# DeltaNet stage of a two-layer hybrid backbone: doubling masks and beside-scaling issued on VectorE instead of GpSimd

## Chip, core and metric

One Trainium2 chip, one of its cores, one program of 38,510 profiled instructions. The metric is the device time of one execution in microseconds (us). Engines: TensorE (PE; its weight loads are PEld), VectorE (DVE), ScalarE (ACT), GpSimd (POOL), SyncE (SP).

## What is computed

The program is two layers of a mixed backbone over 256 latent tokens and 256 context tokens of width 1024: a half feed-forward, a token mixer, a second half feed-forward. The mixer adds three branches; the change is inside one of them, the bidirectional gated DeltaNet. All of its arithmetic is float32. The part that matters, cut from the reference:

```
m = jnp.where(strict, jnp.einsum('bhncd,bhnsd->bhncs', kb, k) * decay, 0.0)
eye = jnp.eye(DN_CHUNK, dtype=jnp.float32)
t_inv = lax.linalg.triangular_solve(eye + m, jnp.broadcast_to(eye, m.shape), left_side=True, lower=True)
u = jnp.einsum('bhncs,bhnse->bhnce', t_inv, v * beta[..., None])
w = jnp.einsum('bhncs,bhnsd->bhncd', t_inv, kb * jnp.exp(gam)[..., None])
...
v_new = u_c - jnp.einsum('bhcd,bhde->bhce', w_c, s)
```

There are 4 heads of dimension 128, two directions (`d` = 0 and 1), and per direction 4 tiles of 128 tokens. A tile holds two chunks of 64 tokens.

## The kernel before

The kernel is written engine by engine; every engine runs its own list in order, and semaphores (`wait_ge`, `then_inc`) tie the lists together. Nothing reorders them. In the DeltaNet stage nothing else of the network runs on TensorE: the stage is a loop over layer `l` (2) and tile step `j` (4), eight passes in all. I call each of the eight a pass; passes 1 to 4 are layer 0, passes 5 to 8 layer 1.

A pass inverts the unit-triangular matrix of a tile for 4 heads and both directions by doubling. `mt` is the masked product of keys with the decay, scaled by `beta`, in 64x64 blocks (128 partitions x 4 heads x 64 columns, so 256 elements in each partition). `X` is the inverse so far and `XT` its transpose. The constant `level` has 6 masks of 64 columns; mask 0 gives the first `X`, masks 1 to 5 pick out of `mt` what level `n` adds. For level `n` and direction `d`:

1. TensorE multiplies `level[d, n % 2]` (the masked `mt`, two buffers per direction) with `X` into PSUM (`TWO[d]`, called Y here; semaphore `y_made`), in `by_block`, 8 products of 64x64.
2. ScalarE copies Y to SBUF (L1075, `y_kept`).
3. TensorE multiplies `XT` with Y (`ONE[d]`, called XY here; `xy_made`).
4. VectorE subtracts XY from `X` (L2026, `x_ready`) and transposes `X` to `XT` (L2030, `xt_ready`).

TensorE's order in a level is Y of d=0, Y of d=1, XY of d=0, XY of d=1. After level 5 the block `beside` (the part of the tile's matrix between its two chunks, 64 partitions) joins the two 64-blocks, and the products with values and state follow.

VectorE begins a pass with, for each direction: L2007 twice and L2008 (products with the decay), L2010 (times `beta`, giving `mt`), L2012 (mask 0), L2015 (identity minus that), L2018 (transpose to `X`). Then come L2021 for both directions (`att`, which also frees the PSUM bank that XY of level 1 writes), then the levels. In levels 1 and 2 VectorE also does one L2042 each (`EG` times `qT`, 512 elements, both operands in SBUF).

GpSimd makes the five masked copies per direction (L772, 128x256, `level_ready`) and scales `beside` (L782, 64x256, twice, `beside_ready`). It starts when `mt_ready` comes and stays two levels ahead: the mask of level n goes into the buffer that Y of level n-2 has read. TensorE waits for both `level_ready` and `x_ready` in front of each Y.

All these tiles are views of one SBUF tensor, which the profile calls `work`; `cst` holds the constants and `small` holds `beta`. TensorE's stage instructions all have line L1538, the helper `mm`.

Of the kernel before, what the change touches and what calls it, by code (L numbers as in the profile page):

```python
# [31 lines left out]
P = 128  # L32
# [359 lines left out]
def backbone(nc, wts, par_d, cst_d, mod_d, x_d, c_d, out_d):  # L392
# [3 lines left out]
    with ExitStack() as ctx:  # L396
# [106 lines left out]
        def C(name, rows=slice(0, P)):  # L503
            at, n = CST[name]
            return cst[rows, at:at + n]
# [243 lines left out]
        @block.gpsimd  # L749
        def _(pool):  # L750
            pool.memset(eps, EPS).then_inc(eps_ready, 1)
            pool.memset(cond32[:, :, :], 0.0).then_inc(cond_zeroed, 1)
            pool.wait_ge(inputs_in, 16 * (DC + 2))
            for l in range(DEPTH):

                pool.wait_ge(att_kept, ATT[l] + width(l) // P * MH)
                for a in (0, 258):
                    last = pool.memset(convin[:, :, :, a:a + 2], 0.0)
                last.then_inc(borders_zeroed, 1)
                pool.memset(T_full[:, :, :], 0.0).then_inc(corners_zeroed, 1)  # L760
                for j in range(4):
                    it = l * 4 + j
                    for n in range(1, LEVELS):
                        for d in range(2):
                            if n == 1:
                                pool.wait_ge(mt_ready[d], it + 1)
                                for ready in beside_ready:
                                    pool.wait_ge(ready, it)
                            elif n > 2:
                                pool.wait_ge(y_made[d], it * LEVELS + n - 2)  # L770
                            mask = C("level")[:, n * BLOCK:(n + 1) * BLOCK].unsqueeze(1).to_broadcast([P, HEADS, BLOCK])
                            pool.tensor_tensor(level[:, d, n % 2, :, :], mt[:, d, :, :], mask,  # L772
                                               ALU.mult).then_inc(level_ready[d], 1)
                    for d in range(2):
                        rows = BEFORE[d]
                        factor = beta[rows, ORDER[d][j], 4 * d:4 * d + 4].unsqueeze(2).to_broadcast([BLOCK, HEADS, BLOCK])
                        pool.wait_ge(kk_read[d], it + 1)
                        for ready in level_ready:
                            pool.wait_ge(ready, (it + 1) * DEPTHS)
                        if d:  # L780
                            pool.wait_ge(beside_ready[0], it + 1)
                        pool.tensor_tensor(beside[rows, d, :, :], beside[rows, d, :, :], factor,  # L782
                                           ALU.mult).then_inc(beside_ready[d], 1)

        @block.scalar
        def _(act):
# [870 lines left out]
        def _(dve):  # L1657
# [156 lines left out]
            for l in range(DEPTH):  # L1814
# [175 lines left out]
                for j in range(4):  # L1990
                    it = l * 4 + j
                    tiles = [ORDER[d][j] for d in range(2)]
                    betas = [beta[:, tiles[d], 4 * d:4 * d + 4] for d in range(2)]
                    for d in range(2):
                        dve.wait_ge(decay_made[d], it + 1)
                        for hd in range(HEADS):
                            c = slice(hd * P, (hd + 1) * P)
                            last = stt(E[:, d, c], ONE[d][:, c], gam[:, d, tiles[d], hd:hd + 1],
                                       C("not_upto" if d == 0 else "not_from"), ALU.subtract, ALU.min)
                        last.then_inc(decay_masked[d], 1)  # L2000
                    for d in range(2):
# [14 lines left out]
                                XT[:, d, :, :], ALU.subtract))  # L2016
                        step.wait()
                        dve.transpose(X[:, d, :, :], XT[:, d, :, :]).then_inc(x_ready[d], 1)  # L2018
                    for d in range(2):
                        dve.wait_ge(kq_made[d], it + 1)  # L2020
                        tt(att[:, d, :], ONE[d][:, :], E[:, d, :], ALU.mult).then_inc(kq_read[d], 1)  # L2021
                    for n in range(1, LEVELS):
                        for d in range(2):
                            dve.wait_ge(xy_made[d], it * DEPTHS + n)
# [3 lines left out]
                            if n < LEVELS - 1:  # L2028
                                dve.wait_ge(x_ready[d], it * LEVELS + n + 1)
                                dve.transpose(XT[:, d, :, :], x).then_inc(xt_ready[d], 1)  # L2030
                            else:
                                if j == 0:
                                    dve.wait_ge(corners_zeroed, l + 1)
                                moved = ONE[d][:, HEADS * BLOCK:].rearrange("p (h c) -> p h c", h=HEADS)
                                for rows in (LOW, HIGH):
                                    last = tt(heads(T_full[rows, d, :])[:, :, rows], XT[rows, d, :, :], moved[rows, :, :],
                                              ALU.subtract)
                                last.then_inc(xt_ready[d], 1)
                        if n < 3:
                            d = n - 1  # L2040
                            dve.wait_ge(gain_exp[d], it + 1)
# [113 lines left out]
```

## Time and profile before

| | |
|---|---|
| median of 3 runs | 2859.64 us (2858.6 to 2860.43) |
| the profiled execution | 2859.57 us |
| its span, first to last instruction | 2857.8 us (1.8 us lie around it) |
| busy: PE, PEld | 2644.8 us (93%), 2095.4 us (73%) |
| busy: DVE, ACT, POOL | 1388.5 us (49%), 994.3 us (35%), 80.3 us (3%) |
| mean granted TensorE clock | 0.952 of full |

"Busy" is time in which an instruction was running on the engine, over its span. A row of the time line reads: start, duration, engine, line, operation, output and inputs, shape, count of merged instructions, and in brackets how long the engine idled before it and who released it. An instruction with no bracket followed its forerunner with no idle time that the profile counts.

### The profile page before, as it was taken

How to read it: one execution, taken by the hardware profiler on the slowest of the kernel's cores; microseconds unless marked ns; L12 is line 12 of the kernel's file. 1: busy time of each engine (PE TensorE's matmuls, PEld its weight loads, DVE VectorE, ACT ScalarE, POOL GpSimd, SP SyncE). 2: the span in 40 equal slices, each digit the busy share in tenths (PEclk: the TensorE clock that was granted, in tenths of full speed). 3: DMA queues.
4: the chain of work that ended last, by engine and by line, in shares of the span. 5: the costliest groups of instructions: out<-in, count | busy, mean ns of one | idle time of the engine just before them, and what ended most of it. 6: DMA issues, size and time to landing. Idle time of an engine off the chain costs nothing.

```text
span 2857.8 us, 38510 instructions
## 1 busy us (share of the span) xinstructions
PE 2644.8 (93%) x16344; PEld 2095.4 (73%) x16344; DVE 1388.5 (49%) x2092; ACT 994.3 (35%) x1541; POOL 80.3 (3%) x108
## 2 busy tenths in 40 slices
PE   4999998989978899989999989999898977889999
PEld 2777777634758877767777768888663767889899
DVE  4333344336776663363332353333435677656654
ACT  2322223323563332223222132222241564344443
POOL 0000000000002200000000000000000002200000
PEclk6999999988988999999999999999997988999999
DMA  5444442100210023424444432222220120024454
GB/s 228 177 177 171 158 157 103 60 30 1 89 59 2 2 90 132 147 74 165 168 169 161 161 126 89 103 96 98 87 89 30 60 74 16 2 101 167 169 185 163
DMA packets 44665, 309.79 MB, mean 108 GB/s; under 512 B 5072, under 2 KB 6224, under 8 KB 7632
## 3 DMA queue, kind: packets, MB, share of 16 engines
q1 hardware_dynamic: 44208, 306.20, 29.2%
q8 instruction: 131, 2.15, 0.3%
q10 hardware_dynamic: 288, 1.14, 0.1%
q14 instruction: 38, 0.31, 0.0%
HBM read 306.27 MB, written 1.05 MB: 108 GB/s over the span
## 4 chain that ended last, share of the span: by engine, by line
PE 84%; DVE 10%; ACT 3%; issue 2%; DMA 1%; SPq 0%; DVEq 0%; ACTq 0%
PE bank L1235 65%; PE bank L1538 7%; PE bank L1251 2%; PE bank L1228 2%; DVE rt L1677 2%; PE bank L1462 2%; PE bank L1484 1%; PE bank L1286 1%; DVE w_lo L1666 1%; DMA ring<-in_wts 1%; PE bank L1264 1%; ACT L816 1%; PE bank L1421 1%; PE bank L1471 1%; DVE u_lo L1706 1%
## 5 line engine op out<-in xcount | busy, mean ns | idle before, releaser
L1666 DVE TENSOR_TENSOR w_lo<-ring,w_hi 128x1024 fp32r<-128x1024 f32 x420 | 511.1, 1225 | 1034.5 <-ACT w_hi L798 1031.3
L1235 PE MATMUL bank<-u_hi,w_hi 128*128 128x512 f32 (+1 forms) x2208 | 818.2, 371 | 83.9 <-DVE w_lo L1666 46.7
L1235 PE MATMUL bank<-u_hi,w_lo 128*128 128x512 f32 (+1 forms) x2208 | 801.8, 363 | 0.0
L1235 PE MATMUL bank<-u_lo,w_hi 128*128 128x512 f32 (+1 forms) x2208 | 799.6, 362 | 0.0
L798 ACT ACTIVATE w_hi<-ring 128x1024 fp32r<-128x1024 f32 x420 | 441.4, 1058 | 956.6 <-PE bank L1235 656.2
L1235 PEld LDWEIGHTS bank<-u_hi,w_hi 128*128 128x128 f32 x2208 | 423.1, 192 | 182.0 <-issue 85.4
L1235 PEld LDWEIGHTS bank<-u_hi,w_lo 128*128 128x128 f32 x2208 | 423.4, 192 | 64.0 <-issue 3.9
L1235 PEld LDWEIGHTS bank<-u_lo,w_hi 128*128 128x128 f32 x2208 | 422.8, 191 | 64.1
L1538 PE MATMUL bank<-work 64*64 64x64 f32 (+1 forms) x3952 | 234.6, 248 | 37.7 <-DVE work L2018 21.4
L1235 PE MATMUL bank<-hidden_hi,w_hi 128*128 128x512 f32 (+1 forms) x704 | 259.3, 368 | 0.0
L1538 PEld LDWEIGHTS bank<-work 64*64 64x64 f32 (+1 forms) x3952 | 222.0, 161 | 49.8 <-POOL work L772 31.7
L1235 PE MATMUL bank<-hidden_lo,w_hi 128*128 128x512 f32 (+1 forms) x704 | 258.2, 367 | 0.0
L1235 PE MATMUL bank<-hidden_hi,w_lo 128*128 128x512 f32 (+1 forms) x704 | 257.7, 366 | 0.0
L1235 PEld LDWEIGHTS bank<-hidden_hi,w_hi 128*128 128x128 f32 x704 | 132.2, 188 | 28.6 <-issue 4.9
L1235 PEld LDWEIGHTS bank<-hidden_lo,w_hi 128*128 128x128 f32 x704 | 132.1, 188 | 24.0
L1235 PEld LDWEIGHTS bank<-hidden_hi,w_lo 128*128 128x128 f32 x704 | 132.3, 188 | 23.6
L1677 DVE RECIPROCAL rt<-rt 128x512 f32<-128x512 f32 (+1 forms) x34 | 104.3, 3067 | 55.3 <-ACT rt L816 55.3
L1251 PE MATMUL bank<-ring,cond 128*32 128x256 f32 x1152 | 83.6, 411 | 21.1 <-DMA ring<-in_wts 21.1
L850 ACT ACTIVATE hidden_hi<-sg 128x512 fp32r<-128x512 f32 (+1 forms) x88 | 50.7, 578 | 132.8 <-DVE sg L1772 132.7
L857 ACT ACTIVATE sg<-bank 128x512 f32<-128x512 f32 (+1 forms) x88 | 46.7, 535 | 116.4 <-PE bank L1235 116.3
L772 POOL TENSOR_TENSOR work<-work,cst 128x256 f32<-128x256 f32 x80 | 68.0, 867 | 417.9 <-DVE work L2010 398.0
L1251 PEld LDWEIGHTS bank<-ring,cond 128*32 128x32 f32 x1152 | 31.6, 114 | 64.1 <-issue 32.4
(190 smaller groups left out, 2523.3 us busy)
## 6 DMA issues: line engine op xcount, KB each, us to landing
ring<-in_wts SPq DMA_DIRECT2D x288, 1024.0 KB, 4.8
h<-in_x SPq DMA_DIRECT2D x8, 256.0 KB, 11.1
par<-in_par ACTq DMA_DIRECT2D x2, 556.0 KB, 5.7
out<-h SPq DMA_DIRECT2D x8, 128.0 KB, 4.0
cst<-in_cst SPq DMA_DIRECT2D x1, 911.5 KB, 10.7
mod_par<-in_mod SPq DMA_DIRECT2D x1, 96.0 KB, 10.0
cond<-in_c SPq DMA_DIRECT2D x1, 8.0 KB, 1.7
```

The costliest lines, as they stand in the source:

```text
L772: pool.tensor_tensor(level[:, d, n % 2, :, :], mt[:, d, :, :], mask, ALU.mult).then_inc(level_ready[d], 1)
L798: act.activation(w_hi[:, b % HALVES, :], half_source(n % RING, part), ACT.Copy).then_inc(weights_rounded, 1)
L816: act.activation(rt[rows, n % 2, 0:w], bank[4 + n % 2][rows, 0:w], ACT.Sqrt, bias=eps[rows, :], scale=1.0 / size).then_inc(roots, 1)
L850: act.activation(h_hi[:, 2 * i + c, 0:w], sg[:, c, 0:w], ACT.Copy).then_inc(hidden_rounded, 1)
L857: act.activation(sg[:, c, 0:w], bank[(q0 + c) % 4][:, 0:w], ACT.Silu).then_inc(drained["a"], 1)
L1228: last = weights.used(pe.matmul(out, lhsT, rhs, start=n == 0, stop=n == len(parts) - 1))
L1235: last = weights.used(pe.matmul(out, lhs[a], rhs[b], start=start and n == 0, stop=stop and n == 2))
L1251: last = pe.matmul(bank[7 - unit % 2][32 * j:32 * j + 32, 0:256], cond32[:, k, :], panel[:, kk, j, :], start=k == 0, stop=k == DC - 1)
L1462: pe.matmul(bank[S_BANKS[a % 4]][:, 0:keys.stop - keys.start], qq[0:QK, hd, t * P:(t + 1) * P], kk[0:QK, hd, keys], start=True, stop=True) ...
L1538: return pe.matmul(out, lhsT, rhs, start=start, stop=stop)
L1666: tt(w_lo[:, b % HALVES, :], half_source(n % RING, part), w_hi[:, b % HALVES, :].bitcast(F32), ALU.subtract).then_inc(panel_left[n % RING] ...
L1677: step(dve.reciprocal(r, r))
```

## The change

GpSimd's whole loop over the passes is taken out. VectorE gets a helper `mask_level(d, n)` that makes the same masked copy, and calls it ten times a pass: masks 1 and 2 before level 1, mask n+2 after VectorE's work of level n (n = 1, 2, 3). The two scalings of `beside` come after VectorE's work of level 4. No other engine's list changes. The rest of the numbers, buffers and semaphores is as before. Line numbers behind the cut are lower in the changed kernel, so L2012, L2015, L2018, L2021, L2026, L2030 and L2042 of before are L1997, L2000, L2003, L2007, L2013, L2017 and L2037 there, and the masks are L1975.

```
@@ gpsimd, in the loop over l
-                for j in range(4):
-                    it = l * 4 + j
-                    for n in range(1, LEVELS):
-                        for d in range(2):
-                            if n == 1:
-                                pool.wait_ge(mt_ready[d], it + 1)
-                                for ready in beside_ready:
-                                    pool.wait_ge(ready, it)
-                            elif n > 2:
-                                pool.wait_ge(y_made[d], it * LEVELS + n - 2)
-                            mask = C("level")[:, n * BLOCK:(n + 1) * BLOCK].unsqueeze(1).to_broadcast([P, HEADS, BLOCK])
-                            pool.tensor_tensor(level[:, d, n % 2, :, :], mt[:, d, :, :], mask,
-                                               ALU.mult).then_inc(level_ready[d], 1)
-                    for d in range(2):
-                        rows = BEFORE[d]
-                        factor = beta[rows, ORDER[d][j], 4 * d:4 * d + 4].unsqueeze(2).to_broadcast([BLOCK, HEADS, BLOCK])
...
-                        pool.tensor_tensor(beside[rows, d, :, :], beside[rows, d, :, :], factor,
-                                           ALU.mult).then_inc(beside_ready[d], 1)
@@ vector, in the loop over j
+                    def mask_level(d, n):
+                        if n > 2:
+                            dve.wait_ge(y_made[d], it * LEVELS + n - 2)
+                        tt(level[:, d, n % 2, :, :], mt[:, d, :, :],
+                           C("level")[:, n * BLOCK:(n + 1) * BLOCK].unsqueeze(1).to_broadcast([P, HEADS, BLOCK]),
+                           ALU.mult).then_inc(level_ready[d], 1)
@@
                         dve.transpose(X[:, d, :, :], XT[:, d, :, :]).then_inc(x_ready[d], 1)
+                        mask_level(d, 1)
                     for d in range(2):
                         dve.wait_ge(kq_made[d], it + 1)
                         tt(att[:, d, :], ONE[d][:, :], E[:, d, :], ALU.mult).then_inc(kq_read[d], 1)
+                        mask_level(d, 2)
                     for n in range(1, LEVELS):
@@ after both directions of level n
+                        for d in range(2):
+                            if n + 2 < LEVELS:
+                                mask_level(d, n + 2)
+                            elif n == 4:
+                                rows = BEFORE[d]
+                                tt(beside[rows, d, :, :], beside[rows, d, :, :],
+                                   betas[d][rows, :].unsqueeze(2).to_broadcast([BLOCK, HEADS, BLOCK]),
+                                   ALU.mult).then_inc(beside_ready[d], 1)
```

The first place is VectorE's list in pass 1 for direction 1, up to the first subtraction of level 1. Before:

```order
L2007 TENSOR_TENSOR work<-bank,work 64x256 [waits decay_exp1,kk_made1]
L2007 TENSOR_TENSOR work<-bank,work 64x256
L2008 TENSOR_TENSOR work<-bank,work 64x256
L2010 TENSOR_TENSOR work<-work,small 128x256 [waits dve_step]
L2012 TENSOR_TENSOR work<-work,cst 128x256 [waits mt_ready1]
L2015 TENSOR_TENSOR work<-cst,work 128x256 [waits dve_step]
L2018 STREAM_TRANSPOSE work<-work 128x256 [waits dve_step]
L2021 TENSOR_TENSOR work<-bank,work 128x512 [waits kq_made0]
L2021 TENSOR_TENSOR work<-bank,work 128x512 [waits kq_made1]
L2026 TENSOR_TENSOR work<-work,bank 128x256 [waits xy_made0]
```

The same place in VectorE's list of the changed kernel (the first row is direction 0's mask 1):

```order
L1975 TENSOR_TENSOR work<-work,cst 128x256
L1992 TENSOR_TENSOR work<-bank,work 64x256 [waits decay_exp1,kk_made1]
...
L2003 STREAM_TRANSPOSE work<-work 128x256 [waits dve_step]
L1975 TENSOR_TENSOR work<-work,cst 128x256
L2007 TENSOR_TENSOR work<-bank,work 128x512 [waits kq_made0]
L1975 TENSOR_TENSOR work<-work,cst 128x256
L2007 TENSOR_TENSOR work<-bank,work 128x512 [waits kq_made1]
L1975 TENSOR_TENSOR work<-work,cst 128x256
L2013 TENSOR_TENSOR work<-work,bank 128x256 [waits xy_made0]
```

A mask now stands ahead of direction 1's first product, one behind its transpose, and one behind each of the two `att` products.

The second place is VectorE's list from level 1's second transpose to level 2's last operation. Before:

```order
L2030 STREAM_TRANSPOSE work<-work 128x256 [waits x_ready1]
L2042 TENSOR_TENSOR work<-work 128x512 [waits gain_exp0]
L2026 TENSOR_TENSOR work<-work,bank 128x256 [waits xy_made0]
L2030 STREAM_TRANSPOSE work<-work 128x256 [waits x_ready0]
L2026 TENSOR_TENSOR work<-work,bank 128x256 [waits xy_made1]
L2030 STREAM_TRANSPOSE work<-work 128x256 [waits x_ready1]
L2042 TENSOR_TENSOR work<-work 128x512 [waits gain_exp1]
```

The same place in the changed kernel:

```order
L2017 STREAM_TRANSPOSE work<-work 128x256 [waits x_ready1]
L1975 TENSOR_TENSOR work<-work,cst 128x256 [waits y_made0]
L1975 TENSOR_TENSOR work<-work,cst 128x256 [waits y_made1]
L2037 TENSOR_TENSOR work<-work 128x512 [waits gain_exp0]
L2013 TENSOR_TENSOR work<-work,bank 128x256 [waits xy_made0]
L2017 STREAM_TRANSPOSE work<-work 128x256 [waits x_ready0]
L2013 TENSOR_TENSOR work<-work,bank 128x256 [waits xy_made1]
L2017 STREAM_TRANSPOSE work<-work 128x256 [waits x_ready1]
L1975 TENSOR_TENSOR work<-work,cst 128x256 [waits y_made0]
L1975 TENSOR_TENSOR work<-work,cst 128x256 [waits y_made1]
L2037 TENSOR_TENSOR work<-work 128x512 [waits gain_exp1]
```

Two masks stand between the second transpose and the next level's first subtraction, and in levels 1 and 2 the 512-element product stands there as well.

## Rows read from the trace of the kernel before

**Rows 1.** The page: busy time by engine, and the chain that ended last.

```profile
PE 2644.8 (93%) x16344; PEld 2095.4 (73%) x16344; DVE 1388.5 (49%) x2092; ACT 994.3 (35%) x1541; POOL 80.3 (3%) x108
...
PE 84%; DVE 10%; ACT 3%; issue 2%; DMA 1%; SPq 0%; DVEq 0%; ACTq 0%
```

**Rows 2.** Busy time by stretch: the DeltaNet stages of layers 0 and 1.

```profile
855.00:1006.00 151.00, 129.80 (x2065) 122.86 (x2065) 94.78 (x222) 56.08 (x148) 38.82 (x48) 0.92 0.01 2
2370.00:2520.00 150.00, 127.88 (x2041) 120.10 (x2042) 94.47 (x220) 58.41 (x151) 38.88 (x48) 0.92 0.03 9
```

**Rows 3.** Time line of pass 3, from the first mask to level 1.

```profile
934.75 0.42 DVE L2012 TENSOR_TENSOR work<-work,cst 128x256 f32<-128x256 f32 x1
934.79 0.96 POOL L772 TENSOR_TENSOR work<-work,cst 128x256 f32<-128x256 f32 x1 [23.93 <-DVE work L2010]
935.21 0.83 DVE L2015 TENSOR_TENSOR work<-cst,work 128x256 f32<-128x256 f32 x1
...
936.59 0.57 PEld L1538 LDWEIGHTS bank<-work 64*64 64x64 f32 x16 [1.21 <-POOL work L772]
...
939.43 0.45 DVE L2018 STREAM_TRANSPOSE work<-work 128x256 f32<-128x256 f32 x1
939.91 1.29 DVE L2021 TENSOR_TENSOR work<-bank,work 128x512 f32<-128x512 f32 x2
939.95 0.61 PEld L1538 LDWEIGHTS bank<-work 64*64 64x64 f32 x16 [2.79 <-POOL work L772]
```

**Rows 4.** VectorE's time line of pass 3: ends of levels 1 to 4.

```profile
943.58 0.65 DVE L2042 TENSOR_TENSOR work<-work 128x512 f32<-128x512 f32 x1
944.79 0.42 DVE L2026 TENSOR_TENSOR work<-work,bank 128x256 f32<-128x256 f32 x1 [0.56 <-PE bank L1538]
...
946.40 1.00 DVE L2042 TENSOR_TENSOR work<-work 128x512 f32<-128x512 f32 x1
947.33 0.42 DVE L2026 TENSOR_TENSOR work<-work,bank 128x256 f32<-128x256 f32 x1
...
949.87 0.42 DVE L2026 TENSOR_TENSOR work<-work,bank 128x256 f32<-128x256 f32 x1 [0.85 <-PE bank L1538]
...
952.88 0.42 DVE L2026 TENSOR_TENSOR work<-work,bank 128x256 f32<-128x256 f32 x1 [1.32 <-PE bank L1538]
```

**Rows 5.** Single lines over all eight passes: duration ns, min/median/max.

```profile
L2015 DVE TENSOR_TENSOR work<-cst,work x16: 826/831/836, 861.3 to 2489.3; 128x256 f32<-128x256 f32 x16
...
L2042 DVE TENSOR_TENSOR work<-work x16: 650/995/1171, 869.8 to 2496.9; 128x512 f32<-128x512 f32 x16
...
L772 POOL TENSOR_TENSOR work<-work,cst x80: 719/814/1176, 860.9 to 2497.4; 128x256 f32<-128x256 f32 x80
```

**Rows 6.** VectorE's time line, end of level 1 in passes 1, 6, 7 and 8.

```profile
871.54 0.42 DVE L2026 TENSOR_TENSOR work<-work,bank 128x256 f32<-128x256 f32 x1 [1.11 <-PE bank L1538]
...
2422.35 1.17 DVE L2042 TENSOR_TENSOR work<-work 128x512 f32<-128x512 f32 x1
...
2456.69 1.08 DVE L2042 TENSOR_TENSOR work<-work 128x512 f32<-128x512 f32 x1
...
2494.37 1.03 DVE L2042 TENSOR_TENSOR work<-work 128x512 f32<-128x512 f32 x1
2495.32 0.41 DVE L2026 TENSOR_TENSOR work<-work,bank 128x256 f32<-128x256 f32 x1
```

**Rows 7.** TensorE's line L1538: until whom its engine sat idle (us, times).

```profile
  POOL work L772: 39.9, 24
  DVE work L2018: 21.4, 8
```

**Rows 8.** Stretches of level 1 in pass 1 and level 2 in pass 3; the clock is the third from the end.

```profile
866.10:869.00 2.90, 2.90 (x54) 2.90 (x56) 2.07 (x5) 0.38 (x1) 2.06 (x3) 0.50 0.00 0
...
944.00:946.50 2.50, 2.40 (x68) 2.11 (x66) 1.87 (x6) 0.78 (x3) 1.88 (x3) 1.00 0.00 0
```

More of the change, by code:

```diff
@@ L760, in _ @@
                 pool.memset(T_full[:, :, :], 0.0).then_inc(corners_zeroed, 1)
-                for j in range(4):
-                    it = l * 4 + j
-                    for n in range(1, LEVELS):
-                        for d in range(2):
-                            if n == 1:
-                                pool.wait_ge(mt_ready[d], it + 1)
-                                for ready in beside_ready:
-                                    pool.wait_ge(ready, it)
-                            elif n > 2:
-                                pool.wait_ge(y_made[d], it * LEVELS + n - 2)
-                            mask = C("level")[:, n * BLOCK:(n + 1) * BLOCK].unsqueeze(1).to_broadcast([P, HEADS, BLOCK])
-                            pool.tensor_tensor(level[:, d, n % 2, :, :], mt[:, d, :, :], mask,
-                                               ALU.mult).then_inc(level_ready[d], 1)
-                    for d in range(2):
-                        rows = BEFORE[d]
-                        factor = beta[rows, ORDER[d][j], 4 * d:4 * d + 4].unsqueeze(2).to_broadcast([BLOCK, HEADS, BLOCK])
[L777 to L781, printed above, removed]
-                        pool.tensor_tensor(beside[rows, d, :, :], beside[rows, d, :, :], factor,
-                                           ALU.mult).then_inc(beside_ready[d], 1)
         @block.scalar
```

## Prediction

> **What bounds the kernel now.** I read the page first, for the bound: TensorE is busy 93% of the span and carries 84% of the chain that ended last; GpSimd is busy 80 us, 3% [rows 1]. So the DeltaNet stage matters only through what TensorE waits for. The view by stretches gives its size: some 150 us in each layer, TensorE busy 130 and 128 of them, VectorE 95 and 94, ScalarE 56 and 58, GpSimd 39 in each, at almost no DMA [rows 2]. Nothing from outside runs beside it, so whatever a pass gains or loses goes straight into the time.
>
> Then the time line of one pass, for what a pass waits for. In its first part TensorE has nothing to do but to wait for VectorE: it starts Y of direction 1 at 939.95, when the transpose L2018 has ended at 939.88 [rows 3]. In the levels the loop is a chain through three engines: subtraction L2026, Y, ScalarE's copy, XY, next L2026. At full clock one turn takes 947.33 - 944.79 = 2.54 us and again 949.87 - 947.33 = 2.54 us [rows 4]. VectorE's own work in a turn (two subtractions, two transposes) leaves it 0.85 us idle ahead of the next L2026, and 1.32 us ahead of level 5's [rows 4]. This idle time is the cover of what the change adds. In levels 1 and 2 the 512-element product L2042 sits in it already: at level 2 nothing is left (L2026 at 947.33 has no idle time before it), at level 1 0.56 us [rows 4].
>
> **The chip's behaviour that the price rests on.** L2012 and L2015 have the same size, 128x256 with both inputs in SBUF. L2012 takes 0.42 us, L2015 0.83 us in all 16 cases (826 to 836 ns) [rows 3, 5]. L2012 starts 0.04 us ahead of GpSimd's mask, L2015 in the middle of it. The mask then takes 0.96 us, where its shortest is 0.719 [rows 3, 5]. The picture: one of the two waits for the other. L2042 fits: 0.65 us where it starts 0.09 us ahead of GpSimd's next pair, up to 1.17 us elsewhere [rows 4, 5, 6]. So I take it that without GpSimd L2015 costs 0.42 and L2042 0.65.
>
> The Trainium skill says the same in "SBUF — State Buffer", section "Who interferes with whom": a VectorE instruction with two SBUF inputs takes its second one through a read interface that it shares with GpSimd, and whoever issues first keeps it. The trace agrees: 0.42 against 0.83.
>
> A mask on VectorE has L2012's form exactly, hence 0.42 us. Where neither needs the other's result, an operation starts about 0.08 us before its forerunner ends: two L2021 take 1.29 us together, and L2026 starts at 947.33 while L2042 ends at 947.40 [rows 3, 4]. No mask is needed by its neighbour, so each takes 0.345 us of VectorE's time, a pair 0.69.
>
> **The change, part by part** (per pass; eight passes).
>
> *GpSimd's list removed.* It frees nothing that is waited for. The trace names L772 as the releaser of TensorE's 24 waits of 39.9 us [rows 7], but the masks were out earlier: direction 1's at about 939.12 (0.96 behind 938.16), TensorE went on at 939.95, just behind L2018; direction 0's mask ended at 935.75, TensorE started at 936.59 [rows 3]. What is gained is the contention: 0.41 us for each L2015 and up to 0.52 for L2042.
>
> *First part.* Direction 0's work loses 0.41 (L2015) and gains a mask of 0.345: direction 1 starts 0.06 us earlier. Again 0.41 against 0.345 for direction 1, so Y of direction 1 comes some 0.13 us earlier. But mask 2 of direction 0 stands ahead of direction 1's `att` product, which frees the bank of direction 1's XY: this ends 0.2 us later than now, and TensorE, which works in order, gives part of the 0.13 back. I book half of 8 x 0.12 us: **-0.5 us**.
>
> *Level 1 to 2.* Two masks are put between the second transpose and the next L2026. In passes 1, 2 and 5 TensorE runs at half clock there (0.50, that is 1.2 GHz [rows 8]) and VectorE idles 1.11 us [rows 6], more than 0.69: nothing. In passes 3 and 4 0.56 us are idle [rows 4]; 0.69 less 0.56 and less the overlap of 0.08 is 0.05 each. In passes 6 to 8 no idle time is left, but L2042 falls from 1.17, 1.08 and 1.03 to 0.65 [rows 6]: 0.69 x 3 - (0.52 + 0.43 + 0.38) = 0.74. Together **+0.8 us**.
>
> *Level 2 to 3.* No idle time in any pass. Masks +0.69, L2042 from 1.00 to 0.65 [rows 4]: +0.34 each, **+2.7 us**. Late by it are L2026 and all that follows in the pass.
>
> *Levels 3 to 4 and 4 to 5.* 0.69 us of masks under 0.85 idle. The two scalings of `beside` have 64 partitions and 256 elements; no VectorE row of this form is shown, the nearest is a mask, 0.42 us, and even with no overlap 0.9 us lie under 1.32 [rows 4]. TensorE needs `beside` only after level 5. Nothing. If the cover were gone they would cost 0.69 and 0.9 a pass.
>
> *Waits.* The new wait on `y_made` is for a Y whose copy is long made when VectorE reaches the mask (its XY has already been subtracted), so nothing queues behind it. No DMA moves.
>
> Sum: -0.5 + 0.8 + 2.7 = +3.0 us. Against the profiled execution's own 2859.57 us (span 2857.8 and 1.8 around it), which lies 0.07 under the median, this gives **2862.6 us**, +0.1%. A measurement of this kernel can tell about 0.2%, 5.7 us, from no change.
>
> The bounds of the unknown terms: first part -1.0 (Y's lead kept) to 0; a mask 0.345 to 0.45 of VectorE's time; L2015 and L2042 between their two observed durations. That is what the rivals price.
>
> **Rivals.**
>
> *A. No overlap: each mask costs 0.45 us* (0.42 and a gap of 0.03 as from 935.17 to 935.21 [rows 3]). For it: every operation that waits for its forerunner has this gap. Against: masks don't. First part 8 x 2 x (0.45 - 0.41) = 0.6; level 1 to 2: 2 x (0.90 - 0.56) + 3 x 0.90 - 1.33 = 2.1; level 2 to 3: 8 x (0.90 - 0.35) = 4.4; level 3 to 4: 8 x 0.05 = 0.4. Sum +7.5: 2867.1 us, slower. It decides from about 0.42 us per mask on.
>
> The Trainium skill has a rule for it: "VectorE: DVE Perf Modes", section "The DRAIN you can't avoid", says that the next operation doesn't start until the pipe is empty, though the section on two instructions with no wait between them lets some start earlier. The trace speaks for the second: 1.29 us for two operations of 0.69.
>
> *B. The long L2015 and L2042 are not GpSimd's doing.* For it: 831 ns is strikingly constant. Against: GpSimd's mask stands at the same place each time, and L2042 varies between 650 and 1171 ns. Then nothing pays for the masks: first part 8 x 0.69, level 2 to 3 8 x 0.69, level 1 to 2 2 x 0.13 + 3 x 0.69 = 13.4 us: 2873.0 us, slower.
>
> *C. TensorE did wait for GpSimd's masks*, as the profile names it [rows 7]. Then its 16 waits of level 1 shrink by 0.96 - 0.42 = 0.54 us each, -8.6 us: 2851.0 us, faster. Against it are the end times worked out above.
>
> *D. The clock moves.* The half clock of level 1 costs pass 1 about 0.65 - 0.08 + 1.11 = 1.68 us of VectorE's slack instead of 0.85, so 0.83 us; the same in passes 2 and 5, and 0.56 + 0.57 - 0.85 = 0.28 in passes 3 and 4. When the passes shift, these low stretches may fall elsewhere: if all went away -3.1 us, while the masks of level 1 would then show in passes 1 to 5 too (5 x 0.34 less the 0.1 booked): 2859.57 + 3.0 - 3.1 + 1.6 = 2861.1 us, or 2859.6 if they don't. The opposite, all eight as low as pass 1, costs 5 x 0.83 - 2 x 0.28 = 3.6 and hides the 0.8 of level 1: 2865.4 us.
>
> **How the numbers follow.** My forecast 0.66 (its own range 2860.5 to 2865), D 0.12, A 0.10, B 0.07, C 0.05. The range goes from 2857.8 to 2868.0: it holds the forecast, nearly all of D and most of A, and leaves out B, C and the edges, 0.2. Faster by over 0.2% is C, 0.05, and some 0.01 of D; slower by over 0.2% is A and B, 0.17; within 0.2% 0.77.
>
> **What the profile after would show.** L2000 (was L2015) at about 0.42 us: right on contention; at 0.83: B. L2037 (was L2042) at 0.65. Masks at 0.38 to 0.42 us, their starts 0.35 apart; 0.45 apart: A. From level 2's first subtraction to level 3's 2.88 us instead of 2.54, then 2.54 again. TensorE's Y of direction 1 about 5.1 us behind L1997's start of direction 0, now 5.20; at 4.6 or less C is right. I would be wrong if VectorE's queue were late in levels 3 or 4 as well, or if the granted clock of the stages left 0.92 by more than 0.02.

## The result and the profile after

The changed kernel takes 2863.9 us (median of 20 runs) against 2859.09 us; the ratio is 1.0016, 95% interval 1.0009 to 1.0023, so 4.6 us slower, between 2.6 and 6.6. One run of each kernel took far longer (3365.81 and 6534.54 us); the ratio leaves them out. The forecast was +3.0 us, with 2857.8 to 2868.0 as its range. The traced execution took 2865.29 us at the same mean clock as before, 0.952.

The page's rows on the engines and on the chain, which answer to [rows 1]:

```profile
PE 2647.8 (92%) x16344; PEld 2095.5 (73%) x16344; DVE 1409.6 (49%) x2188; ACT 994.6 (35%) x1541; POOL 2.6 (0%) x12
...
PE 82%; DVE 11%; ACT 3%; issue 2%; DMA 1%; SPq 0%; DVEq 0%; ACTq 0%
```

VectorE has 21 us more work, GpSimd 78 us less. TensorE's share of the chain fell by two points, VectorE's rose by one. The two stages by stretches, as [rows 2]:

```profile
855.00:1006.00 151.00, 128.67 (x2066) 120.70 (x2066) 105.84 (x270) 56.20 (x147) 0.00 (x0) 0.94 0.01 2
2370.00:2520.00 150.00, 127.40 (x2020) 118.93 (x2021) 106.10 (x270) 56.65 (x146) 0.00 (x0) 0.89 0.03 9
```

The clock is third from the end: 0.94 in layer 0's stretch and 0.89 in layer 1's, both 0.92 before. This is the first sign that the clock has a part in it. But the program comes to layer 1's stage 3.7 us later now, so the same stretch holds more of the half-clock time that lies ahead of it. From the first mask of pass 5 to the last level of pass 8 the two kernels differ by 0.01 only, before first:

```profile
2380.18:2503.40 123.22, 104.55 (x1841) 98.09 (x1842) 85.62 (x199) 47.56 (x128) 38.88 (x48) 0.93 0.01 2
```

```profile
2383.87:2508.80 124.93, 105.97 (x1842) 99.29 (x1842) 95.86 (x247) 47.58 (x128) 0.00 (x0) 0.92 0.01 2
```

The single lines over all passes (ns, min/median/max), as [rows 5]. L2000 is the identity minus mask 0 (L2015 before), L2037 the 512-element product (L2042 before), L1975 the masks:

```profile
L2000 DVE TENSOR_TENSOR work<-cst,work x16: 424/424/427, 861.8 to 2493.6; 128x256 f32<-128x256 f32 x16
...
L2037 DVE TENSOR_TENSOR work<-work x16: 681/685/686, 870.7 to 2502.6; 128x512 f32<-128x512 f32 x16
...
L1975 DVE TENSOR_TENSOR work<-work,cst x80: 381/398/417, 862.6 to 2505.1; 128x256 f32<-128x256 f32 x80
```

With GpSimd gone the strange 831 ns are 424, in all 16 cases, and the product no longer varies between 650 and 1171. That speaks for the two engines having been in each other's way; the experiments below test it.

VectorE's time line of pass 3, first part, as [rows 3]:

```profile
934.35 0.42 DVE L1997 TENSOR_TENSOR work<-work,cst 128x256 f32<-128x256 f32 x1
934.80 0.42 DVE L2000 TENSOR_TENSOR work<-cst,work 128x256 f32<-128x256 f32 x1
935.26 0.45 DVE L2003 STREAM_TRANSPOSE work<-work 128x256 f32<-128x256 f32 x1
935.63 0.38 DVE L1975 TENSOR_TENSOR work<-work,cst 128x256 f32<-128x256 f32 x1
935.94 0.86 DVE L1992 TENSOR_TENSOR work<-bank,work 64x256 f32<-64x256 f32 x2
...
939.33 0.69 DVE L2007 TENSOR_TENSOR work<-bank,work 128x512 f32<-128x512 f32 x1
```

A mask takes 0.31 us of VectorE's time (935.63 to 935.94), not 0.345. The first `att` product starts 4.98 us behind mask 0, before it was 5.16. And the levels of the same pass, as [rows 4]:

```profile
943.09 0.72 DVE L1975 TENSOR_TENSOR work<-work,cst 128x256 f32<-128x256 f32 x2
943.72 0.68 DVE L2037 TENSOR_TENSOR work<-work 128x512 f32<-128x512 f32 x1
944.67 0.42 DVE L2013 TENSOR_TENSOR work<-work,bank 128x256 f32<-128x256 f32 x1 [0.27 <-PE bank L1515]
...
946.28 0.71 DVE L1975 TENSOR_TENSOR work<-work,cst 128x256 f32<-128x256 f32 x2
946.92 0.68 DVE L2037 TENSOR_TENSOR work<-work 128x512 f32<-128x512 f32 x1
947.52 0.41 DVE L2013 TENSOR_TENSOR work<-work,bank 128x256 f32<-128x256 f32 x1
...
950.05 0.42 DVE L2013 TENSOR_TENSOR work<-work,bank 128x256 f32<-128x256 f32 x1 [0.21 <-PE bank L1515]
```

Level 2 to 3 takes 947.52 - 944.67 = 2.85 us instead of 2.54, with no idle time ahead of the subtraction: VectorE is the bound there. Level 3 to 4 is at 2.53 again and has 0.21 us left of the 0.85.

The rest can be counted by starts on VectorE's time line. From the start of mask 0 (direction 0) to the first subtraction of level 5, summed over the eight passes, I get (us):

| | before | after |
|---|---|---|
| mask 0 to level 1 | 57.8 | 56.0 |
| level 1 to 2 | 24.2 | 25.2 |
| level 2 to 3 | 20.3 | 22.8 |
| level 3 to 5 | 44.4 | 44.3 |
| sum | 146.6 | 148.2 |

The passes explain +1.6 us. The spans differ by 5.7. Of this 0.45 us lie ahead of the first mask (which starts at 860.86 us before and 861.31 after), where the two programs are the same; traces of kernels that are the same up to there put it anywhere from 858.75 to 861.61 us, so this is scatter. From the first mask to the end it is 2002.2 us against 1996.9, so +5.3. The rest lies outside of the passes, and most of it in one place: from the first mask of pass 4 to that of pass 5, through the end of layer 0 and the first part of layer 1, where the two kernels do the same work in the same order, it takes 2383.87 - 972.72 = 1411.15 us, and before 2380.18 - 972.55 = 1407.63. The rows of these four starts, the kernel before first:

```profile
972.55 0.42 DVE L2012 TENSOR_TENSOR work<-work,cst 128x256 f32<-128x256 f32 x1
...
2380.18 0.43 DVE L2012 TENSOR_TENSOR work<-work,cst 128x256 f32<-128x256 f32 x1
```

After:

```profile
972.72 0.42 DVE L1997 TENSOR_TENSOR work<-work,cst 128x256 f32<-128x256 f32 x1
...
2383.87 0.42 DVE L1997 TENSOR_TENSOR work<-work,cst 128x256 f32<-128x256 f32 x1
```

Going through this stretch instruction by instruction (ScalarE's records stand in the same order in both), the distance between the traces is constant to 0.1 us (leaving out the copies of weights, which run ahead and swing) but for these places: near 2073 us the changed kernel gains 0.26, near 2217 to 2220 it loses 1.2, near 2328 to 2345 it loses 1.7, and near 2367 another 0.5. At the first of the losses, TensorE's time line of the kernel before:

```profile
2217.05 0.66 PE L1471 MATMUL bank<-cst,work 128*128 128x128 f32 x4
2217.54 1.02 PE L1462 MATMUL bank<-work 96*128 96x512 f32 x2
2218.74 0.66 PE L1471 MATMUL bank<-cst,work 128*128 128x128 f32 x4 [0.17 <-DVE work L1925]
```

And of the kernel after:

```profile
2217.33 1.12 PE L1448 MATMUL bank<-cst,work 128*128 128x128 f32 x4
2218.24 1.91 PE L1439 MATMUL bank<-work 96*128 96x512 f32 x2
2219.94 1.06 PE L1448 MATMUL bank<-cst,work 128*128 128x128 f32 x4
```

The same four products (the first row) take 1.12 us instead of 0.66. The stretches tell why, before first, then after (span, TensorE's busy time, clock, DMA):

```profile
2205.00:2217.00 12.00, 8.03 (x12) 0.50 0.01 1
2217.60:2220.40 2.80, 2.58 (x15) 1.00 0.01 3
```

```profile
2205.00:2217.00 12.00, 8.02 (x12) 0.50 0.00 0
2217.60:2220.40 2.80, 2.80 (x9) 0.50 0.00 0
2222.00:2232.00 10.00, 10.00 (x57) 1.00 0.00 0
```

Both come out of a thin stretch at half clock (0.50, 1.2 GHz: small products between VectorE's roots and rotations) into the attention. Before, the clock is back at full (2.4 GHz) by 2217.6 us, as the attention's first heads run; after, it is still at half to 2220.4 and full only in the next stretch shown. In the traces' clock records this half clock begins at 2176.07 us before and 2176.52 after, and it ends at 2217.03 and 2220.89.

### The profile page after: what moved, and what is told of

The parts are those of the page before. It is cut to its first block, busy times and chain, and to the rows that moved or that the text cites. A ratio compares the mean times of both kernels' runs of the same rounds, so it can differ in the third digit from the quotient of the medians.

```text
span 2863.5 us, 38468 instructions
## 1 busy us (share of the span) xinstructions
PE 2647.8 (92%) x16344; PEld 2095.5 (73%) x16344; DVE 1409.6 (49%) x2188; ACT 994.6 (35%) x1541; POOL 2.6 (0%) x12
## 4 chain that ended last, share of the span: by engine, by line
PE 82%; DVE 11%; ACT 3%; issue 2%; DMA 1%; SPq 0%; DVEq 0%; ACTq 0%
PE bank L1212 65%; PE bank L1515 6%; PE bank L1228 2%; PE bank L1205 2%; DVE rt L1654 2%; PE bank L1439 2%; PE bank L1461 1%; PE bank L1263 1%; DVE w_lo L1643 1%; DMA ring<-in_wts 1%; PE bank L1241 1%; DVE work L2013 1%; PE bank L1448 1%; ACT L793 1%; PE bank L1398 1%
## 5 line engine op out<-in xcount | busy, mean ns | idle before, releaser
L1749 DVE TENSOR_TENSOR sg<-sg,bank 128x512 f32<-128x512 f32 (+1 forms) x88 | 54.0, 617 | 49.4 <-PE bank L1212 49.4
```

Source lines behind the costliest of these rows:

```text
L1749: tt(sg[:, c, 0:w], sg[:, c, 0:w], bank[(q0 + 2 + c) % 4][:, 0:w], ALU.mult).then_inc(drained["v"], 1)
```

## The experiments

The theories. **Q**: the passes decide, VectorE's queue in levels 1 and 2 costs and the end of the contention gains. **S**, later sharper as **L**: the larger part of the loss is the granted clock outside the stage, decided by some tenths of a microsecond in when the program comes to a place. **A**, the rival of L, says that times just add: a delay costs what it lasts. Every run is compared with runs of the kernel before on the same chip.

**The changed kernel again, unchanged.**

> The changed kernel once more, unchanged, to have it beside the others on one chip and to see in a second trace what the eight passes add and what lies outside of them. Theory Q (VectorE's queue in levels 1 and 2 is the cost, contention the gain): the eight passes, from the first mask to level 5's first subtraction, sum to 148 us again (before: 146.6), and level 2 to 3 takes 2.84 us in each. Theory S (the time is lost outside the stage, where stretches of low clock fall otherwise): the part outside of the passes differs from the first trace's by 2 us or more either way. Time: 1.0010 to 1.0023 of before.

1.0018 of before (1.0010 to 1.0027). The passes sum to 148.3 us, level 2 to 3 takes 2.84 to 2.88 in each. And the part outside repeats as well: pass 4 to pass 5 takes 1411.13 us. The two traces' spans differ by 1.55 us, all of it ahead of the first mask; from there to the end both take 2002.2 us. So the loss is no accident of one execution, as theory S had it, but belongs to the program.

**The 512-element products behind level 5**, in the changed kernel:

```
-                        if n < 3:
-                            d = n - 1
-                            dve.wait_ge(gain_exp[d], it + 1)
...
+                    for d in range(2):
+                        dve.wait_ge(gain_exp[d], it + 1)
+                        tt(heads(EG[:, d, :]), ..., ALU.mult).then_inc(gain_ready[d], 1)
                     for d in range(2):
                         dve.wait_ge(fresh_made[d], it + 1)
```

> The changed kernel, with VectorE's two 512-element products (EG times qT) moved from levels 1 and 2 to behind level 5, where VectorE idles 5 us. Theory Q: level 2 to 3 falls from 2.84 to 2.54 us in all eight passes and level 1 to 2 from 2.94 to about 2.6 where the clock is full; 8 x 0.3 + 5 x 0.3 = -4 us against the changed kernel, so about 1.0000 to 1.0005 of before. Theory S: the turns shorten in the same way, but the time stays within 1.5 us of the changed kernel.

1.0011 (1.0002 to 1.0020). Its time line of pass 3:

```profile
942.79 0.42 DVE L2013 TENSOR_TENSOR work<-work,bank 128x256 f32<-128x256 f32 x1 [1.03 <-PE bank L1515]
...
944.40 0.72 DVE L1975 TENSOR_TENSOR work<-work,cst 128x256 f32<-128x256 f32 x2
945.33 0.42 DVE L2013 TENSOR_TENSOR work<-work,bank 128x256 f32<-128x256 f32 x1 [0.21 <-PE bank L1515]
```

Level 2 to 3 is 2.54 us again (2.58 in pass 5), and the passes sum to 145.4 us, 1.2 less than before: inside the stage this kernel beats the old one, as Q says. The step was smaller than Q had it, 2.8 us and not 4, since level 1 to 2 gave 0.6 and not 1.5. Its time is still 0.11% above it, and pass 4 to pass 5 takes 2382.77 - 970.56 = 1412.21 us. Of its two expectations on the time the one of theory S came nearer: the medians are 1.2 us apart (2862.23 and 2863.45). From the first mask to the end the traces differ by 2.0.

**The same move in the kernel before**, with GpSimd still making the masks (the same edit, on the old kernel).

> The kernel before, GpSimd still makes the masks, with the same two products moved behind level 5. It tells whether they alone cost anything. Theory Q: level 2 to 3 was at 2.54 us with them and stays there; level 1 to 2 loses the 0.1 to 0.2 us that three passes lay above it; first part unchanged, L2015 still 0.83 us: -0.5 us, 0.9998 of before. A rival of it (the products cost in the kernel before as well): -2 us or more.

0.9999 (0.9990 to 1.0008), passes 146.5 us (0.1 less, where 0.5 was expected), pass 4 to 5 1407.66. The products were covered as long as the masks were elsewhere; at level 2 to 3 only both together cost.

**Mask 1 on VectorE, the others on GpSimd, products late.**

```
-                    for n in range(1, LEVELS):
+                    for n in range(2, LEVELS):
                         for d in range(2):
-                            if n == 1:
-                                pool.wait_ge(mt_ready[d], it + 1)
+                            if n == 2:
+                                pool.wait_ge(level_ready[d], it * DEPTHS + 1)
...
                         dve.transpose(X[:, d, :, :], XT[:, d, :, :]).then_inc(x_ready[d], 1)
+                        tt(level[:, d, 1, :, :], mt[:, d, :, :],
+                           C("level")[:, BLOCK:2 * BLOCK].unsqueeze(1).to_broadcast([P, HEADS, BLOCK]),
+                           ALU.mult).then_inc(level_ready[d], 1)
```

> VectorE makes only mask 1 (behind its transpose to X), GpSimd masks 2 to 5 and the scaling of beside, starting mask 2 when mask 1 is out; the 512-element products behind level 5. So no operation of VectorE with two SBUF inputs should meet GpSimd in the first part. Theory Q: the first operation after mask 0 falls from 0.83 to 0.42 us, first part 7.15 to 7.24 before, now 7.0; levels 2.54 us at full clock. Sum over eight passes about -1.5 to -2.5 us, 0.9992 to 0.9996 of before. If the 0.83 us were not contention it stays and the first part grows by 0.7 us.

1.0014 (1.0005 to 1.0023), where a gain was expected: a miss on the time. In the stage the contention went as written, and the first part takes 7.0 us:

```profile
932.85 0.42 DVE L2012 TENSOR_TENSOR work<-work,cst 128x256 f32<-128x256 f32 x1
933.31 0.42 DVE L2015 TENSOR_TENSOR work<-cst,work 128x256 f32<-128x256 f32 x1
...
934.60 0.72 POOL L772 TENSOR_TENSOR work<-work,cst 128x256 f32<-128x256 f32 x1 [25.99 <-DVE work L2019]
```

L2015 is at 0.42 us though GpSimd still makes masks, since it no longer makes one at that moment, and GpSimd's mask is at 0.72 instead of 0.96. The passes sum to 145.3 us, 1.3 less than before, a little short of the 1.5 expected at least. But pass 4 to 5 takes 2383.30 - 971.08 = 1412.22. Three kernels with 1411 to 1412, two with 1407.6: time for theory L.

**0.4 us of delay added to the changed kernel**, once, in layer 1:

```
                     dve.wait_ge(roots, n + 1)
+                    if l and kind == "q":
+                        for _ in range(2):
+                            step(dve.tensor_copy(small[:, 206:207], eps))
+                            step.wait()
```

> The changed kernel with 0.3 to 0.4 us of idle work added once: two copies of one column to an unused place, one after the other, on VectorE in layer 1 ahead of the reciprocal of the query roots (about 2174.8 us), where TensorE waits for VectorE. Theory L (the place of the program against the chip's changes of TensorE's clock decides over some 3 us: the traces of all kernels with masks on VectorE come to this point 0.25 to 0.4 us earlier against the clock's edges than before, and lose 1.1 us each at about 2220, 2330 and 2367): the three steps go, the time FALLS by about 2.8 us, to 1.0007 of before. Theory A (times just add): it grows by 0.4 us.

1.0009 (1.0000 to 1.0018), from 1.0018: with work added it came down, and pass 4 to 5 takes 2378.35 - 971.30 = 1407.05 us, 4.1 less than without the copies. Not all of this is gain: the passes sum to 149.4 us, 1.1 more, with more turns at half clock. From the first mask to the end it is 3.3 less. TensorE's row at the attention's start has the short form again:

```profile
2216.93 0.66 PE L1448 MATMUL bank<-cst,work 128*128 128x128 f32 x4
```

**The same delay in the kernel with the late products.**

> The kernel with the 512-element products behind level 5, with the same two copies. Theory L: 3.1 us less than without them, about the time of before (0.9998 to 1.0003). Theory A: 0.4 us more, 1.0012 of before.

0.9998 (0.9989 to 1.0007), from 1.0011; pass 4 to 5 1409.03 us, 3.2 less (3.3 from the first mask to the end).

**0.3 us of work left out of the kernel before**, at the same place (it leaves 48 of the 256 query roots of layer 1 uninverted):

```
-                    dve.reciprocal(r, r).then_inc(head_roots_inverted, 1)
+                    cut = r[:, 0:208] if l and kind == "q" else r
+                    dve.reciprocal(cut, cut).then_inc(head_roots_inverted, 1)
```

> The kernel before, with 0.3 us of work left out at the same place: VectorE's reciprocal of the query roots in layer 1 takes 208 of the 256 columns (the last 48 tokens' roots stay uninverted). Theory L: coming 0.3 us earlier to the clock's edge costs the three steps, the time GROWS by about 2.9 us to 1.0010 of before, with less work. Theory A: 0.3 us less.

1.0011 (1.0002 to 1.0020), with less work and untouched passes (146.7 us). Pass 4 to 5 takes 2381.75 - 970.99 = 1410.76 us, 3.1 more than before (3.3 from the first mask to the end). The attention's second group of four products, in TensorE's time line, has the long form (1.06 us, before 0.66 at 2218.74):

```profile
2217.84 1.06 PE L1471 MATMUL bank<-cst,work 128*128 128x128 f32 x4
```

**The delay in the kernel with mask 1 on VectorE.**

> The kernel with mask 1 on VectorE, masks 2 to 5 on GpSimd and the late products, with the same two copies. Theory L: 2.8 to 3.1 us less than without them, 0.9998 to 1.0003 of before. Theory A: 0.4 us more.

1.0001 (0.9992 to 1.0010), from 1.0014; pass 4 to 5 1407.99 us, 4.2 less (3.5 from the first mask to the end).

**The delay in the kernel before**, as a control.

> The kernel before with the two small copies alone (ahead of the reciprocal of the query roots in layer 1). A control for the runs with them: here the three steps at 2220, 2330 and 2367 us aren't there to begin with. Theory L (place against the clock's edges): nothing to win, 0.3 to 0.4 us more, 1.0001 of before. If the copies themselves did something good, it would fall here too, by 2 us or more.

1.0002 (0.9994 to 1.0011), pass 4 to 5 1408.68, passes 145.8 us; from the first mask to the end 0.1 more than before. The copies do nothing good by themselves.

The traces of all runs can be sorted by one number: how long behind the fall of the clock near 2176 us the attention's first four products start. In six traces it is 40.95 to 41.26 us (the kernel before, as it is, with the late products and with the delay, and the three other kernels with the delay), and there the half clock lasts 40.96 us. In seven it is 40.60 to 40.83 us (the changed kernel twice, its late products, mask 1 on VectorE, the shorter reciprocal, `beside` alone and the contention put back, both told below), and there the half clock lasts 44.37 us. None of the thirteen is out of line. The doubled masks, the last run below, stand apart: the fall itself comes at another place of the program there (39.85 us, and the half clock lasts 40.96).

**Only the scaling of `beside` on VectorE.** GpSimd keeps all its masks; its last loop goes and VectorE gets the two products behind level 4, as in the change.

> One part alone: only the two scalings of beside are made by VectorE (behind level 4), GpSimd still makes all masks. Theory Q: nothing in the passes, level 4 to 5 stays at 3.01 us, first part 7.15 to 7.24. Whether layer 1's mixer comes earlier against the clock's edges I can't say beforehand: if any longer list of VectorE does that, the time is 1.0010 of before, if only the shorter passes do, it is 1.0000.

1.0010 (1.0001 to 1.0020). The passes are those of before (146.8 us). Pass 4 to 5 takes 2382.68 - 971.84 = 1410.84 us. Eight instructions in each layer, all hidden, moved from GpSimd's list to VectorE's, cost most of what the whole change costs (the medians are 3.8 us apart, 5.1 with the whole change). It begins 145 us ahead of the attention, at the last rows of the norm that feeds layer 1's mixer. VectorE's time line of the kernel before:

```profile
2071.19 0.88 DVE L1706 SCALAR_TENSOR_TENSOR u_lo<-sq,mods,u_hi 128x256 fp32r<-128x256 f32 x2
2072.67 0.88 DVE L1706 SCALAR_TENSOR_TENSOR u_lo<-sq,mods,u_hi 128x256 fp32r<-128x256 f32 x2 [0.60 <-ACT u_hi L836]
2073.47 1.22 DVE L1666 TENSOR_TENSOR w_lo<-ring,w_hi 128x1024 fp32r<-128x1024 f32 x1
```

And of the kernel with `beside` alone, where the idle time is 0.25 instead of 0.60:

```profile
2070.46 0.88 DVE L1694 SCALAR_TENSOR_TENSOR u_lo<-sq,mods,u_hi 128x256 fp32r<-128x256 f32 x2
2071.59 0.88 DVE L1694 SCALAR_TENSOR_TENSOR u_lo<-sq,mods,u_hi 128x256 fp32r<-128x256 f32 x2 [0.25 <-ACT u_hi L824]
```

The kernel before, and the three with VectorE's list unchanged in length up to here (late products, shorter reciprocal, delay alone), all show 0.60 or 0.61. All ten traces of kernels with more instructions on VectorE ahead of this place show 0.25 or 0.26. It is a wait of 0.35 us that they don't have, at an instruction that has nothing to do with the change. The same ten also have fewer instructions on GpSimd, and no run separates the two.

The DMA records give a lead. In the four traces with the wait, the instruction behind it is the 1600th of VectorE's records, and a transfer of instructions (8 KB, queue 14) starts 0.67 to 0.70 us behind its start. In all 14 traces such a transfer comes when VectorE has started 1597 to 1601 of them, so with 8 instructions more it lies 2.1 us ahead of this place, with 48 or more 47 us and farther. The rows of the transfer, first of the kernel before (window 2073.3 to 2073.5 us), then of `beside` alone (2069.4 to 2069.6):

```profile
q14 instruction: 1, 0.01, 17.8%
```

```profile
q14 instruction: 1, 0.01, 12.5%
```

So the wait stands where VectorE's own list comes to a block of instructions, and the length of that list moves it away. That a fetch costs the 0.35 us is inferred from the place; no run with instructions added on VectorE alone tests it.

**Contention put back into the changed kernel**:

```
+                for j in range(4):
+                    for d in range(2):
+                        if l + j + d:
+                            pool.wait_ge(unused_made, 8 * l + 2 * j + d)
+                        pool.wait_ge(mt_ready[d], 4 * l + j + 1)
+                        pool.tensor_tensor(unused[:, :], C("level")[:, 0:256], C("level")[:, 64:320],
+                                           ALU.mult).then_inc(unused_made, 1)
```

> The changed kernel, with GpSimd given one useless product of 128x256 constants (both inputs in SBUF, into an unused place) for each direction, started by mt_ready as its first mask was before. It takes no data from the stage and nobody waits for it. Theory Q: VectorE's operation after mask 0 is back from 0.42 to 0.83 us, and the first part of a pass from 7.03 to about 7.8 us; 8 x 0.8 = +6.4 us less what the clock hides, against the changed kernel. Rival B of the prediction (the long time is not GpSimd's doing): 0.42 and 7.03 stay.

1.0042 (1.0029 to 1.0054), an estimated 7 us above the changed kernel's 1.0018, where 6.4 were expected. The first part takes 7.81 to 7.87 us, the passes 156.0 in sum, 7.7 more than the changed kernel's:

```profile
934.44 0.42 DVE L2006 TENSOR_TENSOR work<-work,cst 128x256 f32<-128x256 f32 x1
934.55 0.92 POOL L768 TENSOR_TENSOR unused<-cst 128x256 f32<-128x256 f32 x1 [35.14 <-DVE work L2004]
934.90 0.85 DVE L2009 TENSOR_TENSOR work<-cst,work 128x256 f32<-128x256 f32 x1
```

GpSimd's product shares no data and no semaphore that VectorE waits for with L2009, and L2009 is back at 0.85 us. The Trainium skill has the rule in "SBUF — State Buffer", section "Who interferes with whom": a VectorE instruction with two inputs in SBUF takes the second one through a read interface that it shares with GpSimd, and the order of issue decides who waits. The trace agrees: L2006, which started first, keeps its 0.42.

**Masks behind level 3 made twice**, in the changed kernel (two more products of the same kind ahead of them).

> The changed kernel with both masks behind level 3 made twice. There 0.85 us were idle before, and two masks take 0.69 of them. Theory Q with 0.345 us per mask: four masks take 1.38 us, less the overlap of 0.08 that is 1.30, so level 3 to 4 goes from 2.53 to 2.99 us. With 0.45 us per mask (rival A): 3.4 us.

One run, 2866.98 us. Level 3 to 4 takes 2.91 us in all passes:

```profile
950.09 0.72 DVE L2028 TENSOR_TENSOR work<-work,cst 128x256 f32<-128x256 f32 x2
950.72 0.75 DVE L1975 TENSOR_TENSOR work<-work,cst 128x256 f32<-128x256 f32 x2
951.39 0.42 DVE L2013 TENSOR_TENSOR work<-work,bank 128x256 f32<-128x256 f32 x1
```

Four masks take 951.39 - 950.09 = 1.30 us, 0.325 each. The turn was expected at 2.99 us by this price and at 3.4 by rival A's 0.45, which is out.

## Why the prediction came out right, point by point

The sum was right in its sign and near in size, but partly for another reason than the one it gave. Measured, by its own terms:

*First part*, booked at -0.5 us: -1.8. L2015 fell by 0.41 as written, but a mask behind a transpose takes 0.31 us of VectorE's time and not 0.345, and TensorE gave nothing of the lead back: the first `att` product comes 0.18 us earlier, the first subtraction 0.22. The term was mis-sized: half of the gain was taken off without a row that showed it, and the mask's price was too high. The mechanism holds.

*Level 1 to 2*, booked at +0.8: +1.0. The split by passes was not as written, since the half clock moved to other passes (3, 5 and 8 instead of 1, 2 and 5).

*Level 2 to 3*, booked at +2.7: +2.5, 2.84 us against the 2.88 foreseen. The move of the products to behind level 5 takes this term away entirely, which shows that it is the queue of masks and product together. The product went to 0.685 us, not to 0.65.

*Levels 3 to 5*, booked at nothing: -0.1. The cover of 0.85 held, with 0.21 to spare, and the doubled masks show that it is a cover: some 0.6 us more of work cost 0.38.

*GpSimd's list is waited for by nobody* (against rival C): right. TensorE starts Y of direction 1 at 939.36, 5.01 us behind the first mask; 5.20 before, 5.1 foreseen, 4.6 or less by rival C.

So the passes gave +1.6 us where I had +3.0, and the whole came to +4.6: that the sum lies near the measured time is in part luck, two errors of opposite sign. The step that failed is this one: "Nothing from outside runs beside it, so whatever a pass gains or loses goes straight into the time." It doesn't. Between the starts of pass 4 and pass 5 the changed kernel loses 3.5 us, only 0.2 of it in pass 4 and the rest on unchanged work, the same in a second trace, by the clock. I had the clock as rival D, with a chance of 0.12, for the passes alone. It acted mostly outside the stage, and there it repeats. The runs with 0.4 us of delay show it: three kernels became faster with it (by 0.0009, 0.0013 and 0.0013 of the time), one kernel became slower by 0.0011 with 0.3 us of work less, and the control stayed. In the three pairs with the delay the intervals of the times overlap; the traces settle it, with 3.3, 3.3 and 3.5 us less from the first mask to the end, 3.3 more with the shorter reciprocal and 0.1 more in the control. The prediction's own warning, a stage whose clock leaves 0.92 by more than 0.02, came up in the fixed stretch of layer 1 (0.89), but mostly because the stretch held other work; counted from the first mask it is 0.92 against 0.93.

The chain is then: another split of the instructions over VectorE and GpSimd, a wait of 0.35 us gone at 2072 us, the mixer of layer 1 0.26 us earlier, the clock back at full 3.4 us later in the program at the attention's start, 3.4 us lost there and in the two places after it. The links behind the second are shown by the delays and the shorter reciprocal; the first is shown only as a pattern over the kernels, with the transfer of instructions at VectorE's 1600th as the likely reason of the wait. Outside of this stretch and the passes +0.35 us are left behind level 5 of pass 8, not explained. Nor are the passes' +1.6 all queue: layer 0's came out at -0.1 and layer 1's at +1.7 with the same work. Layer 0 has two turns of level 1 at half clock before and one after, layer 1 one before and two after (3.43 and 3.46 us each, against 2.6 to 3.0 at full clock). At 0.5 to 0.7 us for each such turn, an estimate from these rows, about 0.9 us of the 1.8 between the layers are the clock's; no run separates the rest.

Rival B is refuted by 424 ns in all 16 cases and by the contention put back, rival A by the doubled masks, rival C by the 5.01 us. One slip of the prediction's sums: rival D's second case is 2859.57 + 3.0 - 3.1 = 2859.5, not 2859.6.

None of the versions beats the kernel before beyond what the measurement can tell: the best are 0.9998 and 1.0001, the one with late products and the one with mask 1 alone, each with the delay, though both have 1.1 to 1.3 us less in the passes.

## What to carry to other kernels

Find the idle time that a moved operation will sit in, level by level, and subtract: 0.69 us fit into 0.85 and not into none, where the turn grew by the masks' time less what the product beside them had gained. When two engines seem to take strangely long on equal work, look at what the other one does at that moment: here 0.41 us of every pass and direction were lost to a product with two SBUF inputs on GpSimd. And before a difference of 0.1% is put down to an edit, compare the traces outside of the edit, instruction by instruction: a few tenths of a microsecond earlier or later can cost or save 3 us where TensorE comes out of a thin stretch.

## What was unexpected of the hardware

The granted clock is not mere noise, nor wholly fixed. In all 14 traces the first mask starts 2.28 to 2.52 us behind a rise of the clock, though it comes 858.75 to 861.61 us into the span. Between passes 4 and 5 two traces of one kernel agree to 0.02 us. In layer 0's passes kernels with the same instructions up to there can differ: with the delay, which comes much later, these passes took 74.5 us against 73.8 in the changed kernel, and 73.0 against 73.8 in the kernel before. And arriving earlier can be worse: 0.3 us less work made 2.8 us more time (median 2861.77 against 2858.99), 0.4 us more work made 2.2 to 4.3 us less (2863.45 to 2861.22, 2862.23 to 2858.43, 2862.36 to 2858.03; the medians with and without it were taken on different chips, where the kernel before had 2858.99 and 2858.39).

With a few instructions moved from GpSimd to VectorE, hidden in themselves, a wait of 0.35 us was gone more than 1000 us later (0.60 to 0.25 us idle ahead of the same instruction). It stood at VectorE's 1600th instruction, beside a transfer of instructions that stays with that count.

A two-input product on GpSimd that begins 0.11 us behind VectorE's first product and ends in the middle of its second doubles the second (0.42 to 0.85 us) and takes 0.92 us itself, where a mask of its size took 0.72 us undisturbed.
